# Attention loop of a retention and sliding-window block: VectorE and ScalarE work in two orders, one for even and one for odd pairs

## What is computed

```python
def block(args):            # n: one of 8 blocks of 128 queries
    qn, kn, vn, n = args
    ...
    keys = jnp.concatenate([k_meta, kn], axis=1)     # 16 meta + 2 * 128 keys
    scores = (jnp.einsum('bqhgd,bkhd->bhgqk', qn, keys) - slopes * dist)
    scores = jnp.where(valid, scores, -jnp.inf)
    m = jnp.maximum(jnp.max(scores, axis=-1, keepdims=True), sink)
    p = jnp.exp(scores - m)
    probs = p / (jnp.sum(p, axis=-1, keepdims=True) + jnp.exp(sink - m))
    return jnp.einsum('bhgqk,bkhd->bqhgd', probs, vals)
...
merged = (jax.nn.sigmoid(gr) * (y_ret @ w_ret_branch)
          + jax.nn.sigmoid(gs) * (y_swa @ w_swa_branch))
```

## Time and profile before

| | |
|---|---|
| median of three runs | 1621.34 us (1620.97 to 1622.37) |
| the profiled execution's own time | 1623.07 us |
| its span, first to last instruction | 1621.3 us |
| TensorE busy | 1603.1 us of the span (99%) |
| VectorE, ScalarE, GpSimd busy | 66%, 48%, 25% of the span |
| the attention loop | about 495 to 731 us from the span's start |

### The profile page before, as it was taken

How to read it: one execution, slowest core, us unless ns; L and a number is a source line. 1 busy time by engine, 2 the same in 40 slices (tenths; PEclk the granted TensorE clock), 3 DMA queues, 4 the chain that set the end, 5 groups by cost and what they waited for, 6 DMA issues and landing times.

```text
span 1621.3 us, 22775 instructions
## 1 busy us (share of the span) xinstructions
PE 1603.1 (99%) x7942; PEld 1335.2 (82%) x7942; DVE 1062.5 (66%) x2063; ACT 781.8 (48%) x1615; POOL 406.4 (25%) x584
## 2 busy tenths in 40 slices
PE   9999999999999999999999999999999999999999
PEld 7888888888888787878888888888888888888887
DVE  7984556666566778766564438876666656766675
ACT  6733244455456778772222126655555544444442
POOL 0111011121135888874221000121111222100000
PEclk9999999999999999999999999999999999999999
DMA  8533323265344575667553223354444389733452
GB/s 296 180 102 117 111 104 104 97 215 207 136 154 135 160 182 149 178 163 244 168 197 113 72 66 117 121 178 156 150 143 145 121 306 365 244 98 98 148 183 92
DMA packets 132113, 255.95 MB, mean 158 GB/s; under 512 B 15024, under 2 KB 52320, under 8 KB 132000
## 3 DMA queue, kind: packets, MB, share of 16 engines
q1 hardware_dynamic: 88304, 135.89, 26.4%
q0 software_dynamic: 43408, 118.48, 22.3%
q10 hardware_dynamic: 288, 0.14, 0.0%
HBM read 159.67 MB, written 69.47 MB: 141 GB/s over the span
## 4 chain that ended last, share of the span: by engine, by line
PE 93%; POOL 2%; DVE 2%; DMA 1%; ACT 1%; issue 1%; DVEq 0%; ACTq 0%
PE bank L1226 29%; PE bank L1231 29%; PE bank L1230 29%; POOL PR L1102 2%; PE bank L1529 1%; PE bank L1561 1%; PE bank L1543 1%; DMA PW<-PR 1%; POOL RT L1118 1%; PE bank L1269 0%; PE bank L1661 0%; PE bank L1445 0%; PE bank L1611 0%; DVE WL L2412 0%; PE bank L1578 0%
## 5 line engine op out<-in xcount | busy, mean ns | idle before, releaser
L1226 PE MATMUL bank<-WH,ADH 128*128 128x512 f32 x448 | 174.3, 389 | 0.0
L1230 PE MATMUL bank<-WH,ADL 128*128 128x512 f32 x448 | 174.3, 389 | 0.0
L1231 PE MATMUL bank<-WL,ADH 128*128 128x512 f32 x448 | 174.3, 389 | 0.0
L1102 POOL TENSOR_SCALAR PR<-PR,RC 128x272 f32<-128x272 f32 (+1 forms) x128 | 142.9, 1349 | 36.7 <-DVE RC L2978 36.7
L2338 ACT CAST ADH<-ARAW 128x512 fp32r<-128x512 f32 x112 | 69.6, 621 | 170.9 <-PE bank L1231 156.8
L3234 DVE TENSOR_TENSOR ADL<-ARAW,ADH 128x512 fp32r<-128x512 f32 x112 | 77.5, 692 | 97.0 <-ACT ADH L2338 97.0
L1226 PE MATMUL bank<-HN,WH 128*128 128x512 f32 x344 | 138.0, 401 | 0.0
L1231 PE MATMUL bank<-HN,WH 128*128 128x512 f32 x344 | 135.9, 395 | 0.0
L1230 PE MATMUL bank<-HN,WL 128*128 128x512 f32 x344 | 135.7, 394 | 0.0
L1226 PE MATMUL bank<-SOPH,WH 128*128 128x512 f32 x256 | 99.8, 390 | 0.0
L1231 PE MATMUL bank<-SOPL,WH 128*128 128x512 f32 x256 | 99.6, 389 | 0.0
(11 more groups left out here) (392 smaller groups left out, 4327.2 us busy)
## 6 DMA issues: line engine op xcount, KB each, us to landing
ARAW<-uop SPq DMA_DIRECT2D x112, 256.0 KB, 3.4
uop<-US POOLq DMA_DIRECT2D x64, 256.0 KB, 2.9
WRAW<-in_w_up SPq DMA_DIRECT2D x15, 1024.0 KB, 6.2
PW<-PR SPq DMA_DIRECT2D x56, 272.0 KB, 2.6
RAW<-in_w_in SPq DMA_DIRECT2D x52, 256.0 KB, 4.4
uop<-UA POOLq DMA_DIRECT2D x48, 256.0 KB, 3.2
proj<-SA POOLq DMA_DIRECT2D x36, 256.0 KB, 2.3
RT<-proj POOLq DMA_DIRECT2D x8, 1024.0 KB, 7.2
```

The costliest lines, as they stand in the source:

```text
L1102: pr = pool.tensor_scalar(keys, keys, RC[:, b, hl:hl + 1], None, ALU.mult)
L1226: mm = pe.matmul(bank, ahi, bhi, start=first, stop=False, skip_group_check=onto)
L1230: pe.matmul(bank, alo, bhi, start=False, stop=False, skip_group_check=onto)
L1231: return pe.matmul(bank, ahi, blo, start=False, stop=last, skip_group_check=onto)
```

## The change

Four things:

- In odd steps below 64, VectorE does `top`, `lo_p`, `inverse` and only then the rest; in even steps it does `lo_p` before `top`, and `inverse` stays where it was.
- In odd steps ScalarE does `take_p`, `take_next_q`, `weigh`, and then `take_y`, the `hi_*` casts and the splits. In even steps only one split stands ahead of `weigh` instead of two.
- GpSimd's accumulating store of group G moves from step 2G+7, after the scaling of an even pair, to step 2G+8, after that of an odd pair, and ahead of the table and key/value loads. The loop is two steps longer for it.
- The tiles of slabs 4 and 5 are split at gate steps 57, 58, 60, 61, 63, 64, 66 and 68 of the slab before, not at 56 to 63. That is for slab 4: step 9 (tile 0), 10 (1, 2), 11 (3), 12 (4, 5), 13 (6), 14 (7); for slab 5: step 37 (0, 1), 38 (2), 39 (3), 40 (4, 5), 41 (6), 42 (7). Slab 6 is split where it was.

```diff
+SPLIT_AT = (57, 58, 60, 61, 63, 64, 66, 68)
...
         slab, k = SLAB_D + i // 64, i % 64
-        if 56 <= k < 60 or k >= 60 and slab + 1 < SLAB_E:
+        if slab > SLAB_D and k + 64 in SPLIT_AT:
+            out.append((slab, SPLIT_AT.index(k + 64)))
+        if slab + 1 < SLAB_E:
+            if k in SPLIT_AT:
+                out.append((slab + 1, SPLIT_AT.index(k)))
+        elif 56 <= k < 60:
             out.append((slab + 1, k - 56))
...
-            for T in range(STEPS + 2):
+            for T in range(STEPS + 4):
...
                     pr.then_inc(pn_rdy, 1)
+                if T >= LAG + 5 and T % 2 == 0:
+                    G = (T - LAG - 5) // 2
+                    pool.wait_ge(yc_done[G % 2], 32 * (G // 2 + 1) + (16 if G % 2 else PL0))
+                    for par in range(2):
+                        pool.dma_start(y_place(G, par), y_part(G, 1, par), accum_op=ALU.add)\
+                            .then_inc(yf_done[G % 2], 16)
...
-                if T >= LAG + 4 and T % 2 == 1:
-                    G = (T - LAG - 4) // 2
...
                     take_p(T - LAG)
-                if T >= LAG + 2 and T % 2 == 1:
-                    take_y((T - LAG - 2) // 2)
+                if T % 2 == 1:
+                    if T in NEXT_Q:
+                        take_next_q(*NEXT_Q[T])
+                    if T < NPAIR:
+                        weigh(T)
+                    if T >= LAG + 2:
+                        take_y((T - LAG - 2) // 2)
...
-                if T in NEXT_Q:
+                if T in NEXT_Q and T % 2 == 0:
                     take_next_q(*NEXT_Q[T])
...
-                for slab, k in splits[:2]:
+                for slab, k in splits[:1]:
                     split_hi(slab, k)
-                if T < NPAIR:
+                if T < NPAIR and T % 2 == 0:
                     weigh(T)
-                for slab, k in splits[2:]:
+                for slab, k in splits[1:]:
                     split_hi(slab, k)
...
-                if T < NPAIR:
+                if T < NPAIR and T % 2 == 1:
                     top(T)
                 if LAG <= T < NPAIR + LAG:
                     lo_p(T - LAG)
+                if T < NPAIR and T % 2 == 0:
+                    top(T)
...
+                if T < NPAIR and T % 2 == 1:
+                    inverse(T)
...
-                if T < NPAIR and not (T % 8 == 0 and T // 8 + 1 < NB):
+                if T < NPAIR and T % 2 == 0 and not (T % 8 == 0 and T // 8 + 1 < NB):
                     inverse(T)
```

## The result

The changed kernel takes 1642.01 us (median of four runs, 1640.24 to 1643.98); the kernel before took 1621.15 us in four runs beside them. The ratio is 1.0127, 95% interval 1.011 to 1.0145: 20.6 us slower, where I had forecast 1 us and a range that ended at +6.2. The profiled execution took 1640.24 us.

A forecast was written before the change was run, and what follows sets the result against it. TensorE, busy 99% of the span, was taken as the bound. Terms -4.9 + 1.7 + 3.35 + 1.7 - 1.0 = +0.85 us gave 1623.9 us profiled, 1622.2 on the median; range 1614 to 1627.5.

The forecast's parts named there:

- It fits by 0.3 us ... I take nothing: Store landing at +8.6 us before `take_y` two steps on at +8.9: no cost, 2.8 us as far end.
- Rival C: Stores landing near 6.9 us make ScalarE wait every other step, TensorE behind it: +3 to +8 us, 1625 to 1630; chance 0.06.
- Small waits together: 6.4 - 1.5 = 4.9 us gained: TensorE's small waits at `values` and transposes away from the splits go, less 1.5 us for VectorE's lag in four blocks.
- Its transposes are three steps away, so this is hidden: Even pair's reciprocal comes some 1.1 us later, but its transposes are over 10 us away: no cost.
- rival A: The orders win: VectorE's lag in steps 8 to 15 and 37 to 43 vanishes; -9.2 us, 1612; chance 0.30.
- The spread: Late split tiles at gate steps in slabs 4 and 5: 1.7 and 3.35 us lost, plus 1.7 for a low clock.
- Rival B: Eighth tile: VectorE's lag adds 0.8 us at steps 14 and 42, clock falls at both; +4.2 us, 1625.5; chance 0.24.
- The low clock: TensorE at the lower clock for one stretch behind slab 5's 3.7 us idle time: 1.7 us lost.
- The end: End of the loop: pair 63 scaled before group 28's store, `PW` about 2 us earlier; 1.0 us gained, best 1.8.
- The signs I named: TensorE's L1226 waits of 2 and 3.7 us, no waits before `values` or for odd `PW`, low clock near 647, none near 727.
- the orders with the end: Small waits on TensorE, 4.9 us gained, and the loop's end, 1.0 us gained.

The follow-up runs named there:

- after_other: Full change, but the accumulating store reads a constant tile and the copy of y waits only for SyncE's half, against the kernel before: 1632.31 us, ratio 1.0065.
- lo_first: Kernel before with only VectorE's even-step order changed (`lo_p` ahead of `top`): 1621.1 us, ratio 1.0.
- spread_67: Kernel before with only the splits spread, the last tile at gate step 67 instead of 68: 1619.86 us, ratio 0.9994.
- old_store: Full change with GpSimd's accumulating store back in its old place, against the kernel before: ratio 1.0079, +12.8 us.

## Why the prediction was wrong

- **The failed step, first: "It fits by 0.3 us ... I take nothing"** for the store's lateness. Measured 7.8 to 10.0 us within the change (10 by `after_other`), against a far end of 2.8. Rival C had the wait, at 0.06 and at most 8 us, but for landings near 6.9 us, which did not come. Three faults. I set a median landing (3.8 us) against a slack of 0.3, and the way to it was longer too. Counted from the odd pair's scores in the kernel after, its scaling ended at +4.94 us (median of 29 groups) where I had +4.15, and the second of the two stores landed 4.5 us after its issue (4.1 is the median of both, 5.9 the longest), so at +10.1 where I had +8.6. The issue 0.65 us after the scaling was right. I priced the rest per group as 0.1 us, where 10 groups wait 1.1 us each. And I took ScalarE's 0.6 us before the next `PTH` for a cushion, without asking what else stands behind the copy: in step 8n + 3 the keys' cast, for which VectorE stands ahead of `PTL`.
- **The failed step, second: "Small waits together: 6.4 - 1.5 = 4.9 us gained".** Its half on `values` was right (4.5 us gained with the orders alone, as forecast). Its half on the transposes was wrong in sign: I had 1.9 gained and 1.5 lost, the trace has 6.1 lost (0.5 in the net before, 6.6 with the orders alone). "Its transposes are three steps away, so this is hidden" looked at the even pair's own way; the lateness goes through VectorE's order to `PTL` of the next step, and in four blocks only by my count, in far more of them in the trace (27 idle times ahead of `PTL` with `lo_first`, 3 before).
- **Not priced at all:** the reciprocal's early place on VectorE (+6.0 us alone) and ScalarE's order (+5.4 alone). I counted only what they release. With all orders together the slabs' steps lose 3.3 us more than before at `values` and transposes, where rival A had their lag vanish.
- **The spread** was the right mechanism and nearly the right size: least waits of 2.1 and 3.4 us forecast, 2.12 and 3.36 measured by starts; 6.75 us in all with a low clock, against 4.9 alone and 6.5 to 8.7 in the change. Rival B's point, 9.1 us together, was not quite reached.
- **The low clock** I charged once at slab 5, and it fell there (behind 3.52 us of idle time); the one at slab 4 stayed away, behind 1.81 and 1.73 us; the one at the end, near 727 before, which I took to be gone, fell behind 2.39 us. In the profiled executions the net was nothing, two before and two after. Over all runs it wasn't: the mean granted clock of 0.9965 is worth about 4 of the 20.6 us.
- **The end** was forecast at 1.0 us gained and lost 0.9 (4.5 to 5.4). With the orders alone it gained 1.4, and with the constant tile about as much. It is the first failed step again: I had a copy of y late by 1.3 us there, it was late by 2.42, and with the low clock behind it the gain was gone.
- The signs I named: L1226 (L1232 in the new code) waiting near 2 and 3.7 us was there (1.73 and 3.52 us idle, 1.9 and 3.7 by starts), the low clock came behind slab 5's opening (near 655) as named, but also at the end, where I had none, no wait for odd pairs' `PW` was wrong (3.0 us in 4), and the 0.2 us before `values` went in the orders alone, but in the full change came back as the copies of y.

Term by term, each part on top of the ones before it: the orders with the end, forecast -5.9 us, measured +4.1; the spread, forecast +6.75, measured +8.7; the store, forecast 0, measured +7.8. That is off by 10.0, 2.0 and 7.8 us, the 19.8 us between +0.85 and +20.6. The split depends on the order in which the parts are added: alone they sum to far more (4.1, 4.9 and 58.4), as the new orders hold down what the store does.

## What to carry to other kernels

When a store is moved behind other work, follow its landing to whoever must reuse the buffer, and from there through that engine's order back to the store: if the way closes into a circle, its length against the bounding engine's period is the price, at every turn. A slack set against the median landing covers only half of them. An instruction moved ahead on an in-order engine can lose behind it what it gains at its own consumer: 5.0 us gained and 5.9 lost for the even steps' subtraction, nothing gained and 6.0 lost for the odd steps' reciprocal. Count the ready work that it now stands in front of. And where an engine is at 65% of the time but in a chain with two others, an order may be tuned to the other orders, as here: take one part at a time.

## What the runs showed of the hardware

Accumulating stores of 64 KB from GpSimd took 2.5 us at the least, 4.1 in the median and 5.9 at the most from issue to landing in the kernel after; SyncE's plain half of the same size took 2.1. The Trainium skill, "DMA: Bandwidth & Descriptors", section "Anatomy of one DMA — SWDGE (gpsimd) path", puts the fixed part near 2 us; only the shortest of these landings is near that.

Idle time did not decide the clock by its length alone. In the kernel before it fell behind 1.76 and 1.86 us and not behind 2.10. In the one after it did not fall behind 1.81 (step 12) and 1.73 us (step 15), but behind 3.52 and 2.39. With the spread alone it fell behind the 1.94 us ahead of slab 4's last tile, and the opening of slab 5, which waited 3.19 us, shows no lower clock at all:

```profile
540.63 0.50 PE L1232 MATMUL bank<-HN,WH 128*128 128x512 f32 x1 [1.94 <-DVE WL L2418]
```

```profile
540.00:560.00 20.00, 19.03 (x110) 16.06 (x111) 13.72 (x44) 12.27 (x33) 13.51 (x15) 0.91 0.54 139
...
640.00:660.00 20.00, 16.41 (x104) 13.69 (x104) 14.72 (x49) 13.68 (x38) 16.76 (x20) 1.00 0.58 147
```

In the kernel with both orders alone, the stretch 520 to 540 has a mean of 0.83, two stretches' worth of loss in one:

```profile
520.00:540.00 20.00, 16.01 (x83) 13.40 (x82) 16.00 (x46) 14.21 (x36) 15.07 (x16) 0.83 0.50 130
```

A fall costs about 1.7 us. The stretches show none in `spread_67`, two in the kernel before and four in `old_store` (0.91, 0.91 and 0.83 in three of them). So a difference of that size between two single profiles of this kernel isn't by itself the edit's. The mean clock over several runs says more: 0.9965 in the four runs of the full change, 0.999 in the kernel before.
